# Modulation sums behind the down products, and three first weight tiles made a stage ahead, in a two-block transformer kernel on Trainium2

## What is computed

```python
def first_block(x, ...):
    h = rmsnorm(x, norm_mix[l])
    proj = h @ w_in[l]
    ...
    y_a = retention(rq, rk, rv, rg, ret_gn_g[l]) @ w_ret_o[l]
    y_b = nsa(...) @ w_nsa_o[l]
    merged = jax.nn.sigmoid(ga) * y_a + jax.nn.sigmoid(gb) * y_b
    x = x + merged @ w_out[l]
    x = x + conv_ffn(rmsnorm(x, norm_ffn[l]), w_up[l], conv_w[l], conv_b[l], w_down[l])

def second_block(x, c, w_ada, b_ada, ...):
    ada = jax.nn.silu(c) @ w_ada[l] + b_ada[l]
    sh_m, sc_m, g_m, sh_f, sc_f, g_f = jnp.split(ada, 6, axis=-1)
    ...
    x = x + g_m[:, None, :] * (jnp.concatenate([y_rwkv, y_s5], axis=-1) @ w_out[l])
```

## Time and profile before

| | us |
|---|---|
| median of 3 runs | 4089.57 (4086.43 to 4089.7) |
| the profiled execution | 4083.01 |
| its span, first to last instruction | 4081.2 |
| TensorE busy | 3589.8 (88%) |
| VectorE busy | 1737.7 (43%) |
| GpSimd busy | 1046.7 (26%) |
| ScalarE busy | 838.6 (21%) |

### The profile page before, as it was taken

The page is one execution under the profiler, slowest core; times in us unless marked ns, Lnnn a source line. Parts: engine busy times, 40 slices in busy tenths (PEclk is TensorE's granted clock), DMA queues, the critical chain, the costliest instruction groups (busy, mean ns, idle before and its releaser), DMA issues. The chain is left out here.

```text
span 4081.2 us, 56633 instructions
## 1 busy us (share of the span) xinstructions
PE 3589.8 (88%) x23457; PEld 2969.4 (73%) x23457; DVE 1737.7 (43%) x2716; ACT 838.6 (21%) x1237; POOL 1046.7 (26%) x506
## 2 busy tenths in 40 slices
PE   5999999866689978999999969968894689999997
PEld 4878888655577767788888857847783568888886
DVE  4842221215677753555555553324432323232324
ACT  2111110100233411211111130135332131111112
POOL 3333333302121023321212133322221232212121
PEclk9999999955699989999999979979996889999998
DMA  3433332330000031232222116420001111111111
GB/s 98 141 127 110 114 114 78 120 104 22 17 8 8 1 124 42 73 121 75 83 73 85 58 42 176 115 78 19 19 3 62 52 47 57 43 50 57 36 51 42
DMA packets 306417, 279.43 MB, mean 68 GB/s; under 512 B 21134, under 2 KB 276672, under 8 KB 305272
## 3 DMA queue, kind: packets, MB, share of 16 engines
q1 hardware_dynamic: 279520, 200.62, 16.5%
q10 hardware_dynamic: 25980, 74.48, 5.1%
q0 software_dynamic: 720, 1.51, 0.1%
HBM read 217.71 MB, written 58.85 MB: 68 GB/s over the span
## 5 line engine op out<-in xcount | busy, mean ns | idle before, releaser
L702 POOL TENSOR_TENSOR ffn_wlo<-ffn_raw,ffn_whi 128x1024 fp32r<-128x1024 f32 x88 | 211.3, 2403 | 1077.8 <-ACT ffn_whi L875 1024.6
L197 PE MATMUL up<-h_hi,ffn_whi 128*128 128x512 f32 x1408 | 438.9, 393 | 20.2 <-POOL h_lo L396 19.7
L197 PE MATMUL up<-h_lo,ffn_whi 128*128 128x512 f32 x1408 | 436.1, 391 | 0.0
L197 PE MATMUL up<-h_hi,ffn_wlo 128*128 128x512 f32 x1408 | 435.8, 391 | 0.0
L197 PEld LDWEIGHTS up<-h_hi,ffn_whi 128*128 128x128 f32 x1408 | 264.0, 189 | 79.3 <-POOL h_lo L396 13.5
L197 PEld LDWEIGHTS up<-h_lo,ffn_whi 128*128 128x128 f32 x1408 | 266.2, 189 | 55.9
L197 PEld LDWEIGHTS up<-h_hi,ffn_wlo 128*128 128x128 f32 x1408 | 265.7, 189 | 55.8
L186 POOL TENSOR_TENSOR proj_whi<-proj_raw,ones 128x1024 fp32r<-128x1024 f32 x69 | 137.4, 1991 | 600.0 <-PE acc L1168 389.2
L1168 PE MATMUL acc<-h_hi,proj_whi 128*128 128x512 f32 x816 | 264.0, 405 | 9.2 <-POOL h_lo L396 9.2
L1168 PE MATMUL acc<-h_lo,proj_whi 128*128 128x512 f32 x816 | 253.1, 391 | 0.0
L1168 PE MATMUL acc<-h_hi,proj_wlo 128*128 128x512 f32 x816 | 252.7, 391 | 0.0
(11 more groups left out here) (563 smaller groups left out, 6741.6 us busy)
## 6 DMA issues: line engine op xcount, KB each, us to landing
proj_raw<-w_in SPq DMA_DIRECT2D x69, 512.0 KB
projT<-proj_stage ACTq DMA_DIRECT2D x51, 512.0 KB, 2.6
ffn_ada_raw<-w_ada SPq DMA_DIRECT2D x24, 1024.0 KB, 5.0
ffn_raw<-w_up SPq DMA_DIRECT2D x44, 512.0 KB
ffn_draw<-w_down SPq DMA_DIRECT2D x11, 1024.0 KB, 6.9
ffn_raw<-ffn_w_gate SPq DMA_DIRECT2D x22, 512.0 KB
ffn_raw<-ffn_w_up SPq DMA_DIRECT2D x22, 512.0 KB
ffn_draw<-ffn_w_down SPq DMA_DIRECT2D x11, 1024.0 KB, 4.9
```

Source lines behind the costliest of these rows:

```text
L197: last = nc.tensor.matmul(acc[:, t, :], w[:, k, w_cols], x[:, k, t * HALF:(t + 1) * HALF], start=(k == 0 and i == 0), stop=(k == k_tiles - ...
L702: nc.gpsimd.tensor_tensor(w_lo[i][:], raw[i][:], w_hi[i][:], ALU.subtract).then_inc(s[f"up_split{i}"], 1)
```

## The change

`gemm` can take its unit 0 as already split (`first`, the number of the buffer in which it lies) and can load and split one more tile behind its own units (`then`). The weight buffers become three shared pairs, `mem.weights`, at the same addresses. The projections load and split ret_out's first tile as unit 51, nsa_out that of mix_out as its unit 8, and glu that of mix2_out as its unit 4. The programs of SyncE, GpSimd and TensorE in `gemm` are written out for all units in place of loops. In the first feed-forward, the sums of (c - 1, 1) go behind the down products of c - 1 and into dn0 (`where`), with a wait for dn0's last read; the others stay in dn1. The first unit's sums (0, 0) move behind the first down products too, and VectorE's takes move behind `add_down`. The waits of the down products are now for the takes of the turn before.

```diff
--- before.py
+++ after.py
@@ -124,22 +124,26 @@
         body(n // 2, 0)
-def gemm(nc, mem, name, n_units, k_tiles, weight, rhs, epilogue, at, extra="", norm=None):
-    raw = [mem.at(f"{name}_raw{b}", at + 4 * b, [P, KD, P]) for b in range(2)]
-    w_hi = [mem.at(f"{name}_whi{b}", at + 8 + 4 * b, [P, KD, P], F32R) for b in range(2)]
-    w_lo = [mem.at(f"{name}_wlo{b}", at + 16 + 4 * b, [P, KD, P], F32R) for b in range(2)]
+def gemm(nc, mem, name, n_units, k_tiles, weight, rhs, epilogue, extra="", norm=None, first=None, then=None):
+    order = (1, 0) if first == 1 else (0, 1)
+    raw, w_hi, w_lo = ([x[b] for b in order] for x in mem.weights)
     names = "weight_loaded0 weight_loaded1 hi_done0 hi_done1 split_done0 split_done1 products_done0 products_done1 "
     names += "acc_read0 acc_read1 vector_step scalar_step stored0 stored1 loaded0 loaded1 epilogue_a0 epilogue_a1 epilogue_b0 epilogue_b1 " + extra
     names += RMS_SEMS if norm else ""
     banks = [(n, [P, NH, HALF], F32) for n in ("acc0", "acc1", "tot")[0:3 if norm else 2]]
     hi, lo = rhs
+    last_unit = n_units + (1 if then is not None else 0)
+    ready_units = 0 if first is None else 1
+    def nth(u):
+        return u // 2 + 1 - (ready_units if u % 2 == 0 else 0)
+    assert then is None or n_units % 2 == 0
     with phase(nc, names, banks) as (block, s, ps):
         acc = [ps["acc0"], ps["acc1"]]
         if norm:
@@ -147,36 +151,38 @@
         @block.sync
         def _(sp):
-            def load(p, b):
-                sp.wait_ge(s[f"split_done{b}"], p)
-                sp.dma_start(raw[b][:, 0:k_tiles, :], weight(2 * p + b)).then_inc(s[f"weight_loaded{b}"], 16)
-            pairs(sp, n_units, load)
+            for u in range(ready_units, last_unit):
+                b = u % 2
+                if u >= 2 and nth(u) > 1:
+                    sp.wait_ge(s[f"split_done{b}"], nth(u) - 1)
+                tiles, view = (KD, then) if u == n_units else (k_tiles, weight(u))
+                sp.dma_start(raw[b][:, 0:tiles, :], view).then_inc(s[f"weight_loaded{b}"], 16)
         @block.gpsimd
         def _(pool):
-            def split(p, b):
-                pool.wait_ge(s[f"weight_loaded{b}"], 16 * p + 16)
-                pool.wait_ge(s[f"products_done{b}"], p)
-                pool_high(nc, w_hi[b][:, 0:k_tiles, :], raw[b][:, 0:k_tiles, :], mem.one).then_inc(s[f"hi_done{b}"], 1)
-                pool.wait_ge(s[f"hi_done{b}"], p + 1)
-                nc.gpsimd.tensor_tensor(w_lo[b][:, 0:k_tiles, :], raw[b][:, 0:k_tiles, :], w_hi[b][:, 0:k_tiles, :],
+            for u in range(ready_units, last_unit):
+                b = u % 2
+                tiles = KD if u == n_units else k_tiles
+                pool.wait_ge(s[f"weight_loaded{b}"], 16 * nth(u))
+                if u >= 2:
+                    pool.wait_ge(s[f"products_done{b}"], u // 2)
+                pool_high(nc, w_hi[b][:, 0:tiles, :], raw[b][:, 0:tiles, :], mem.one).then_inc(s[f"hi_done{b}"], 1)
+                pool.wait_ge(s[f"hi_done{b}"], nth(u))
+                nc.gpsimd.tensor_tensor(w_lo[b][:, 0:tiles, :], raw[b][:, 0:tiles, :], w_hi[b][:, 0:tiles, :],
                                         ALU.subtract).then_inc(s[f"split_done{b}"], 1)
-            pairs(pool, n_units, split, norm.pool_part if norm else None)
+                if norm and u == 1:
+                    norm.pool_part(pool)
         @block.tensor
         def _(pe):
-            first = [True]
-            def products(p, b):
-                pe.wait_ge(s[f"split_done{b}"], p + 1)
-                pe.wait_ge(s[f"acc_read{b}"], p)
-                ready = (lambda k: norm.ready(pe, k)) if norm and first else None
-                first.clear()
+            for u in range(n_units):
+                b = u % 2
+                if u >= ready_units:
+                    pe.wait_ge(s[f"split_done{b}"], nth(u))
+                if u >= 2:
+                    pe.wait_ge(s[f"acc_read{b}"], u // 2)
+                ready = (lambda k: norm.ready(pe, k)) if norm and u == 0 else None
                 three_pass(nc, acc[b], w_hi[b], w_lo[b], hi, lo, k_tiles, ready=ready).then_inc(s[f"products_done{b}"], 1)
-            pairs(pe, n_units, products)
         epilogue(block, s, acc, ps)
@@ -729,40 +735,49 @@
                     last = three_pass(nc, dn[b], d_hi, d_lo, g_hi, g_lo, 2, slice(n * P, (n + 1) * P))
                     last.then_inc(s[f"down_done{b}"] if n < KD - 1 else s["chunk_done"], 1)
+            where = 0
             def column_sums(u, b, n):
                 pe.wait_ge(s[f"ada_done{b}"], n + 1)
                 for i in range(2):
-                    last = nc.tensor.matmul(dn[1][:, 0, 2 * b + i:2 * b + i + 1], ada_part[b][:, i * P:(i + 1) * P], env["ones"][:, 0:1],
+                    last = nc.tensor.matmul(dn[where][:, 0, 2 * b + i:2 * b + i + 1], ada_part[b][:, i * P:(i + 1) * P], env["ones"][:, 0:1],
                                             start=True, stop=True)
                 last.then_inc(s[f"ada_summed{b}"], 1)
             summed = modulation(column_sums)
             def turn(c):
+                nonlocal where
+                early = isinstance(c, int) and c
                 up_products(c, 0)
+                if w_ada is not None and early != 1:
+                    pe.wait_ge(s["ada_taken"], 4 if early == 2 else 2 * c + 1)
+                down_products(c - 1)
                 if w_ada is not None:
-                    pe.wait_ge(s["ada_taken"], 1 if isinstance(c, int) and c == 1 else 4 if isinstance(c, int) and c == 2 else 2 * c + 1)
+                    where = 0
+                    pe.wait_ge(s["down_read0"], 4 * c)
+                    if early == 1:
+                        summed(0, 0)
                     summed(c - 1, 1)
-                    pe.wait_ge(s["ada_taken"], 2 if isinstance(c, int) and c == 1 else 2 * c + 2)
-                down_products(c - 1)
                 up_products(c, 1)
                 if w_ada is not None:
+                    where = 1
                     pe.wait_ge(s["down_read1"], 4 * c)
                     summed(c, 0)
             up_products(0, 0)
             up_products(0, 1)
-            if w_ada is not None:
-                summed(0, 0)
             turn(1)
             turn(2)
             with pe.Fori(3, C) as c:
                 turn(c)
             if w_ada is not None:
                 pe.wait_ge(s["ada_taken"], 2 * C + 1)
+            down_products(C - 1)
+            if w_ada is not None:
+                where = 0
+                pe.wait_ge(s["down_read0"], 4 * C)
                 summed(C - 1, 1)
-                pe.wait_ge(s["ada_taken"], 2 * C + 2)
-            down_products(C - 1)
         @block.vector
         def _(dve):
@@ -832,21 +847,27 @@
-                if isinstance(u, int) and u in (2, 4):
+                if isinstance(u, int) and u in (0, 2, 4):
...
-                nc.vector.tensor_tensor(prm[:, bass.ds(2 * u + ADA, 2)], dn[1][:, 0, 2 * b:2 * b + 2],
+                nc.vector.tensor_tensor(prm[:, bass.ds(2 * u + ADA, 2)], dn[where][:, 0, 2 * b:2 * b + 2],
...
+            where = 0
...
+                nonlocal where
...
+                add_down(c - 1)
+                where = 0
+                if isinstance(c, int) and c == 1:
+                    taken(0, 0)
...
-                add_down(c - 1)
...
+                where = 1
@@ -856,14 +877,14 @@
                 dve.wait_ge(s["c_done"], 1)
             modulate(0, 0)
             hidden(0, 1)
-            taken(0, 0)
             modulate(0, 1)
             turn(1)
             turn(2)
             with dve.Fori(3, C) as c:
                 turn(c)
+            add_down(C - 1, True)
+            where = 0
             taken(C - 1, 1)
-            add_down(C - 1, True)
             add_squares(KD - 2)
             add_squares(KD - 1)
@@ -1009,11 +1028,12 @@
-                b, t = u % 2, PROJ_UNITS[u]
+                b = u % 2
...
-                c = GATE_COL if t == GATE else t * P + (N_GATE if t >= GA else 0)
-                sp.dma_start(raw[b][:], w_in[:, :, c:c + P]).then_inc(s[f"weight_loaded{b}"], 16)
+                t = PROJ_UNITS[u] if u < N else None
+                c = GATE_COL if t == GATE else (t or 0) * P + (N_GATE if (t or 0) >= GA else 0)
+                sp.dma_start(raw[b][:], then if u == N else w_in[:, :, c:c + P]).then_inc(s[f"weight_loaded{b}"], 16)
@@ -1055,7 +1075,7 @@
-            for u in range(2, N):
+            for u in range(2, N + 1):
@@ -3421,7 +3441,7 @@
-    gemm(nc, mem, "glu", 4, 4, columns(ins["s5_w_glu_2"], 4), (z_hi, z_lo), epilogue, 104)
+    gemm(nc, mem, "glu", 4, 4, columns(ins["s5_w_glu_2"], 4), (z_hi, z_lo), epilogue, then=columns(ins["w_out_2"], KD)(0))
@@ -3546,6 +3566,8 @@
+    mem.weights = [[mem.at(f"{n}{b}", at + 4 * b, [P, KD, P], F32 if n == "raw" else F32R) for b in range(2)]
+                   for n, at in (("raw", 104), ("whi", 112), ("wlo", 120))]
@@ -3562,19 +3584,19 @@
```

(12 more changed lines are left out.)

10 lines of the change are left out of this document (4 added, 6 removed).

## The result

| us | before | after |
|---|---|---|
| median, runs side by side | 4089.64 (4086.43 to 4090.91) | 4057.57 (4056.45 to 4060.29) |
| the profiled execution | 4083.01 | 4057.40 |
| its span | 4081.2 | 4055.2 |

The ratio is 0.9924, 95% interval 0.9907 to 0.9941: 32.1 us off the median where 41.7 were forecast. The time lies 0.4 inside the upper end of the range. What is to be explained is a shortfall of about 10 us.

The account below looks back on a forecast made before the run. TensorE, busy 88% of the span, was taken as the bound, so only its waits counted. Savings of 21.5 + 13.6 + 6.6 = 41.7 us took the median of 4089.6 to 4048, range 4039 to 4058.

Parts of the forecast that it names:

- Part 1: First weight tiles made a stage ahead for ret_out, mix_out and mix2_out: 8.3 + 5.5 + 7.7 = 21.5 us saved.
- 2.3 + 0.4: End of nsa_out: 2.3 us for one block of VectorE by the extra split, 0.4 for tiles sharing DMA engines.
- the lock rival: End of nsa_out: both halves of the extra split block VectorE; mix_out gives 3.2 us, time 4050; chance 0.15.
- Parts 2 and 3: First feed-forward: sums moved behind down products save 13.6 us; the last turn's earlier down products save 6.6.
- the middle value: Feed-forward's last turn: 6.6 us taken, bounds 4.5 to 7.5; a clock fall loses up to 3.0.
- slower than before: Written-out product loops: TensorE's program arrives too slowly, each of 26 units pays; at 2.5 us each 4113; chance 0.03.
- The step from the profiled execution to the median: Whole kernel: the median lies 6.6 us above the profiled execution; the same saving was taken off it, giving 4047.9.

Follow-up runs that it names:

- after + 138: The changed kernel with 138 TensorE instructions that only find a wait already met, at the start of RWKV's program; 4040.52 us (0.9891 of the kernel before).
- after + 106: The changed kernel with 106 TensorE instructions that only find a wait already met, at RWKV's start; first run 4041.69 us (0.9884 of before), again 4044.46 (0.9893).

## Why the prediction was right and where it was wrong

**Part 1 held.** ret_out gave 8.4 (9.1 at its end, 0.7 of it from the projections) for 8.3. TensorE started at 723.25, for 724.1. For mix_out 5.5 was said, and it gave 5.1. From the first product of nsa_out to that of mix_out TensorE took 60.3 us (1458.56 to 1518.83 before) and now 55.2:

```profile
1445.81 1.22 PE L203 MATMUL acc<-h_hi,whi 128*128 128x512 f32 x2 [8.53 <-POOL wlo L171]
...
1501.01 1.19 PE L203 MATMUL acc<-merged_hi,whi 128*128 128x512 f32 x2 [9.15 <-PEq L75]
```

Of that, 8.3 is the earlier start behind nsa_out's last tile, and the price in nsa_out was 3.2 where 2.3 + 0.4 was said. The line that was to show the block, L2178, now L2198 (ns min/median/max):

```profile
L2198 DVE TENSOR_TENSOR nsa_out_stage<-nsa_out_stage,nsa_out_other x8: 1224/1316/3396, 1455.1 to 1496.5; 128x1024 f32<-128x1024 f32 x8
```

One instance was held for 2.2 beside the wide split, once and not twice, so in this trace the lock rival didn't come. The Trainium skill, SBUF — State Buffer, section "SBUF: two separate sides", lets each of the split's two operations block VectorE; this trace shows one block. But it did come in two of the traces with the tiles made ahead, after + 138 and the first after + 106. There two VectorE operations in a row were held, as here in after + 138 (alone they take 0.69 and 1.23), and from nsa_out's first product to mix_out's it was 57.6 and 57.3, so mix_out gave about 3, the rival's 3.2:

```profile
1487.62 2.15 DVE L2200 TENSOR_SCALAR merged_hi<-nsa_out_stage 128x1024 f32 x1 [0.15 <-DVE nsa_out_stage L2198]
1489.90 3.21 DVE L2202 TENSOR_TENSOR merged_lo<-nsa_out_stage,merged_hi 128x1024 f32 x1
```

That is two of eleven traces, for a chance of 0.15.

mix2_out started 8.4 sooner and ended 7.9 sooner, where 7.7 was said: the clock rose at about 3174.3, 3.0 after the start, so less was lost than feared.

**Parts 2 and 3 held.** The stage gave 20.4 for 20.2. A turn of 66.29 for 66.3, a last wait of 3.65 for 3.5. The clock did fall on the last turn, as the middle value assumed (a stretch of the kernel after, columns as in the earlier trace rows):

```profile
2333.00:2334.00 1.00, 1.00 (x4) 0.71 (x4) 0.93 (x3) 0.00 (x0) 0.00 (x0) 0.50 0.00 0
2334.00:2335.00 1.00, 1.00 (x5) 0.82 (x4) 0.94 (x2) 0.00 (x0) 0.00 (x0) 0.69 0.00 0
```

With 8.4, 5.1, 20.4 and 7.9 the terms measured 41.8 for a sum of 41.7. That it is so close is luck too, since single terms are off by up to 0.4.

**The step that failed is the sum's silent one: that stages which the change doesn't touch keep their time.** The mechanism was on the table, in the rival "slower than before": the program, written out, arrives too slowly. It was costed in the wrong place. It asked whether the written-out units themselves would pay, and answered from the projections, straight code without idle. But a product there takes TensorE 0.23 us (10.9 for 48), while a dense run of RWKV does sixteen in 0.68, 0.04 each; a piece lasts 28 us there and 6.5 on average here (415.5 / 64), less in the dense runs. The written-out units do pay nothing. What they do is shift everything behind them by 182 instructions against the pieces. The price falls due three stages behind mix_out, in the one stage whose program is consumed as fast as it comes: 12.7 us in the traces of kernels with this change's tiles, and 8 to 13 at the medians. A rival with 13 would have been 4048 + 13 = 4061, outside the range.

The size is borne out at the medians. At equal places of the pieces, the change is worth 4099.13 - 4056.92 = 42.2 (both bad), 4086.6 - 4044.3 = 42.3, 4085.0 - 4044.9 = 40.1 and 4081.9 - 4044.5 = 37.5 (both good): 40.5 on average for 41.7. The last was to be 41.7 within 3 and misses that by 1.2; it lies in the band of 32 to 38 that was named for a shortfall with another part. Each of the ratios it rests on is known only to 4 to 7 us, so these runs can't tell whether something of 1 to 4 us is left, which may be the busier RWKV left open above. At unequal places it is 32.1, 29.2 and 34.7.

The step from the profiled execution to the median ("nothing in the sum depends on that difference") did no harm to the forecast, but it misled the first comparison of traces: 6 of the 21 us that RWKV seemed to lose were chance, 4 of them the first trace's good luck and 2 the second one's bad luck.

A version that beats both kernels: the change with 74, 106 or 138 idle instructions ahead of RWKV, or with TensorE's loop kept: 4040.5 to 4044.9, against 4052.5 to 4057.6 for the change as it is.

## What to carry to other kernels

Ask of an edit that lengthens an engine's program what runs behind it, not only in it: if some stage consumes that program quickly, its pieces will end elsewhere, and the place alone was worth 8 to 13 us at the medians here. When an untouched stage changes its time, count the instructions done at each unreleased stall; equal counts in kernels that reach the stage at different times speak for the program, and a few idle instructions under an existing wait both prove it and repair it. Before comparing two traces stage by stage, see where each stands among its kernel's runs.

## What the runs showed of the hardware

TensorE's program arrived in packets of 16.4 KB, one for about 126 products with their weight loads. Where one ended in a dense run of 64x64 products TensorE often stood for 0.6 to 3.2 us, and went on 1.2 to 1.7 us after the next packet had landed (98 stalls in eighteen traces). Such stalls came at the same products in each trace of one kernel, with one more or fewer in some. An instruction that only finds its wait met took about 0.11 us in a long row of them, and ten of them in a dense run cost at most 0.6 us of idle. Seven waits of 2.5 us cost 31 us: 17.4 of waiting and 11.3 of busy time, with the granted clock low for 10.2 us around each of the three longest. Stalls of 0.9 to 1.9 us at three places were followed by a fall of the clock within 3.3 us in all seven traces that have them.
